# A mixture-of-experts kernel's first gather taken from fp32 rows, its router run stream by stream, and prefetch hints set ahead of its jumps

## The reference

```python
def hier_moe(h, w_coarse, w_fine, w1, w3, w2):
    x = h.reshape(b * l, d)
    p_coarse = softmax(x @ w_coarse)          # 4 groups
    p_g, g_sel = top_k(p_coarse, 1)           # one group for each token
    fine_g = (x @ w_fine).reshape(-1, 4, 8)[that group]   # 8 experts in it
    top_v, top_i = top_k(fine_g, 2)           # two experts for each token
    w_top = softmax(top_v) * p_g
    gates = ...                               # tokens x 32 experts, two entries a row
    hid = silu(x @ w1[e]) * (x @ w3[e])
    y = sum over e of (hid * gates[:, e]) @ w2[e]
```

## Time and profile before

| | us |
|---|---|
| median of 3 runs | 1395.68 (1394.09 to 1396.05) |
| the profiled execution, whole | 1395.73 |
| its span on the core | 1393.9 |
| MoE of layer 0, from the router's end to the last sum | about 369 to 705 |
| MoE of layer 1 | about 1043 to 1377 |
| PE busy | 1303.1 (93%) |
| DVE busy | 1001.1 (72%) |
| ACT busy | 737.4 (53%) |

### The profile page before, as it was taken

How to read it: one execution, slowest core, us unless ns; L and a number is a source line. 1 busy time by engine, 2 the same in 40 slices (tenths; PEclk the granted TensorE clock), 3 DMA queues, 4 the chain that set the end, 5 groups by cost and what they waited for, 6 DMA issues and landing times.

```text
span 1393.9 us, 17455 instructions
## 1 busy us (share of the span) xinstructions
PE 1303.1 (93%) x6480; PEld 1031.3 (74%) x6480; DVE 1001.1 (72%) x1130; ACT 737.4 (53%) x700; POOL 54.2 (4%) x89
## 2 busy tenths in 40 slices
PE   4999999999889999999979999999987999999994
PEld 1768777887677787887757777788776778788773
DVE  0646566677578888888877556666855888888887
ACT  1443453553456666667753444345434666676773
POOL 1300000001000000000020000000000000000000
PEclk8899999989879999999989999899986999999998
DMA  9977653326758999999966767343334899999991
GB/s 356 324 257 283 224 176 122 124 92 266 278 194 292 359 328 327 322 336 344 359 201 224 263 244 247 121 129 105 122 149 144 301 331 329 334 319 335 345 348 75
DMA packets 96563, 349.54 MB, mean 251 GB/s; under 512 B 8612, under 2 KB 12096, under 8 KB 80080
## 3 DMA queue, kind: packets, MB, share of 16 engines
q1 hardware_dynamic: 87504, 295.12, 59.7%
q0 software_dynamic: 8960, 53.16, 10.9%
HBM read 345.58 MB, written 3.70 MB: 251 GB/s over the span
## 4 chain that ended last, share of the span: by engine, by line
PE 71%; DVE 17%; DMA 4%; ACT 3%; issue 2%; DVEq 2%; SPq 1%; ACTq 0%
PE bank L863 67%; DVE wl L1687 9%; PE bank L866 4%; ACT wh L1597 2%; DMA raw<-in_moe_w 2%; DMA first<-in_w_ada 1%; DMA adaw<-in_w_ada 1%; DVE merged L1687 1%; DVE tmp L1687 1%; DVE x L1687 1%; DVE hid L2362 1%; SPq L708 0%; DVE gv L1687 0%; DVE xgl L2335 0%; DMA raw<-in_w_ada 0%
## 5 line engine op out<-in xcount | busy, mean ns | idle before, releaser
L1687 DVE TENSOR_TENSOR wl<-raw,wh 128x2048 fp32r<-128x2048 f32 (+1 forms) x268 | 610.4, 2278 | 148.5 <-ACT wh L1390 85.9
L1597 ACT ACTIVATE wh<-raw 128x2048 fp32r<-128x2048 f32 x192 | 367.4, 1916 | 62.7 <-PE bank L863 45.8
L863 PE MATMUL bank<-wh,xgh 128*128 128x512 f32 x512 | 213.7, 417 | 10.3 <-DVEq L2336 7.1
L863 PE MATMUL bank<-wh,xgl 128*128 128x512 f32 x512 | 206.1, 402 | 0.0
L863 PE MATMUL bank<-wl,xgh 128*128 128x512 f32 x512 | 205.7, 402 | 0.0
L863 PE MATMUL bank<-wh,hTh 128*128 128x512 f32 (+1 forms) x480 | 195.9, 408 | 9.5 <-ACT merged L1413 4.2
L1390 ACT ACTIVATE wh<-raw 128x2048 fp32r<-128x2048 f32 (+1 forms) x76 | 142.3, 1872 | 101.9 <-PE bank L863 62.1
L863 PE MATMUL bank<-wl,hTh 128*128 128x512 f32 (+1 forms) x480 | 191.2, 398 | 0.0
L863 PE MATMUL bank<-wh,hTl 128*128 128x512 f32 (+1 forms) x480 | 190.4, 397 | 0.0
L863 PEld LDWEIGHTS bank<-wh,xgh 128*128 128x128 f32 x512 | 99.2, 194 | 30.6 <-issue 11.0
L863 PEld LDWEIGHTS bank<-wh,hTh 128*128 128x128 f32 x480 | 94.8, 197 | 31.6 <-DVE wl L1687 5.9
(11 more groups left out here) (285 smaller groups left out, 1602.8 us busy)
## 6 DMA issues: line engine op xcount, KB each, us to landing
raw<-in_moe_w SPq DMA_DIRECT2D x256, 512.0 KB, 5.0
raw<-in_moe_w SPq DMA_DIRECT2D x64, 1024.0 KB, 6.1
raw<-in_w_in SPq DMA_DIRECT2D x52, 1024.0 KB, 6.5
adaw<-in_w_ada POOLq DMA_DIRECT2D x32, 1024.0 KB, 7.1
raw<-in_w_branch SPq DMA_DIRECT2D x12, 1024.0 KB, 5.2
raw<-in_w_ada SPq DMA_DIRECT2D x8, 1024.0 KB, 10.8
raw<-in_w_o SPq DMA_DIRECT2D x8, 1024.0 KB, 4.9
first<-in_w_ada SPq DMA_DIRECT2D x4, 1024.0 KB, 16.8
```

The source lines that it names most:

```text
L863: return behind(nc.tensor.matmul(*args, **kw))
L1597: tally(A_(wh[c][:, :], raw[:, r, :], ACT.Copy), part_high[c])
L1687: return V.tensor_tensor(o, a, b, op)
```

## The change

Three things. **The first gather**: ACT copies the turned-back rows as fp32 into a new tile `x2` (it overlaps `ygh`, `ygl`, not yet in use), PE gathers group 0 from `x2` with fp32 matmuls (16, in two steps, one for each half of the channels), ACT rounds the gathered bank into `xgh` and DVE subtracts it from the same bank into `xgl`. up(0) waits for each half apart. `x2h` is then copied from `x2` by ACT behind the gather, and `x2l` is written by DVE inside experts 1 and 2; the gathers of groups 1 to 3 use them as before. DVE's `lower` of piece 0 moves from ahead of the router to behind `selg`, ACT's `convert` of piece 1 moves ahead of the jump, and DVE lowers piece 2 ahead of expert 0's `hid`. **The router** multiplies half of stream 0 before stream 1 is turned, and both `turn_back`s come ahead of the rank matmuls. **The hints**: `rounds` is written with explicit jumps, each with a prefetch hint some instructions ahead of it (three experts ahead of the end on PE and ACT, ahead of the router's copy on DVE).

```diff
+FIRST_GATHER = {0: (UP_BANK, 0), 1: (TURN_BANK, 0), PREP - 1: (SUM_BANK, 0)}
+        LATE = 3
@@ rounds
             if straight:
-                with eng.If(more < 1):
-                    stream(single, 0, True)
-                with eng.Else():
-                    both()
+                eng.br_cond(more < 1, one, two)
+                one_round()        # ends: leave = eng.br(done); leave.branch_hint(single.late)
+                two_rounds()
             else:
...
+                eng.br_cond(more > 0, two, one).branch_hint(early)
+                two_rounds()
+                one_round()
@@ PE
                 next_ada(2, 6)
+                bank_free(pe, l, "rt")
+                pe.wait_ge(s0_act, 3 * l + 2)
+                route(0, 0, 4)
                 turn_x(l, "x2T", (1,))
                 next_ada(6, 8)
+                pe.wait_ge(s0_act, 3 * l + 3)
+                route(0, 4, 8)
+                pe.wait_ge(s1_dve, 2 * l + 2)
+                route(1, 0, 4)
+                pe.wait_ge(s1_act, 2 * l + 2)
+                fills(route(1, 4, 8), "rt")
                 turn_back(0)
+                turn_back(1)
                 pe.wait_ge(onehot_ready, l + 1)
...
                 fills(ins, "rank")
-                turn_back(1)
@@ PE, gather
+                    if g == 0 and j < 2 and rnd == 0:
+                        pe.wait_ge(x2_rows, 4 * l + 3 + j)
+                        for i in range(4):
+                            for s in range(2):
+                                a = x2[:, s, (4 * j + i) * P:(4 * j + i + 1) * P]
+                                ins = mm(bank[b][:, i * P:(i + 1) * P], a, selg[:, s, :].bitcast(F32), start=s == 0, stop=s == 1)
@@ PE, up
-                        if e == 0:
-                            pe.wait_ge(xg_act, N_G.moe(l, rnd, g) * 2 + 2)
-                            pe.wait_ge(xg_dve, N_G.moe(l, rnd, g) * 2 + 2)
                         for h in range(2):
+                            if e == 0:
+                                pe.wait_ge(xg_act, N_G.moe(l, rnd, g) * 2 + h + 1)
+                                pe.wait_ge(xg_dve, N_G.moe(l, rnd, g) * 2 + h + 1)
@@ ACT
-                        A_(x2h[:, s, h * 512:(h + 1) * 512], t[:, :], ACT.Copy).then_inc(x2_high, 1)
+                        frees(A_(x2[:, s, h * 512:(h + 1) * 512], t[:, :], ACT.Copy), f"x2{s}{h}")
+                        act.drain().then_inc(x2_rows, 1)
+                convert(Tally(act), 0, 1)
...
                     gathered(0, 0)
                     gathered(0, 1)
-                    piece(1)
+                    piece(2)
                     if rnd == 0:
+                        for s in range(2):
+                            A_(x2h[:, s, :], x2[:, s, :], ACT.Copy)
+                            act.drain().then_inc(x2_high, 1)
                         grown(1)
-                    piece(2)
@@ DVE
-                lower(Tally(dve), 0, 0)
+                early = dve.mark_branch_hint_location()
                 t = bank_full(dve, l, "rt")
...
                 choose(0, 0).then_inc(sel_ready, 1)
-                for s in range(2):
-                    for h in range(2):
...
-                        frees(tt(x2l[:, s, hs], t[:, :], x2h[:, s, hs].bitcast(F32), ALU.subtract), f"x2{s}{h}")
+                lower(Tally(dve), 0, 0)
...
+                        if g == 0 and j < 2:
+                            dve.wait_ge(xg_act, N_G.moe(l, rnd, 0) * 2 + j + 1)
+                            tally(tt(xgl[0][part], bank[b][:, :].rearrange("p (c t) -> p c t", c=4), xgh[0][part].bitcast(F32),
+                                     ALU.subtract), free[b])
+                            tally(drain(), xg_dve)
...
+                    gathered(0, 0)
                     piece(1)
-                    gathered(0, 2)
-                    gathered(0, 3)
+                    gathered(0, 1)
                     if rnd == 0:
                         finish_routing()
                         weigh(tally, 0)
+                        piece(2)
                     gathered(0, 4)
@@ DVE, expert i
+                        if rnd == 0 and i in (1, 2):
+                            s = i - 1
+                            dve.wait_ge(x2_high, 2 * l + s + 1)
+                            tt(x2l[:, s, :], x2[:, s, :], x2h[:, s, :].bitcast(F32), ALU.subtract)
+                            drain().then_inc(x2_ready, 1)
```

More of the change, by code:

```diff
@@ L273, in turn_order @@
 def turn_order():
-    order = [("gather", 0, 1), ("gather", 0, 3)]
+    order = [("gather", 0, 1)]
     for i in range(NE):
@@ L401, in hybrid_backbone @@
         (q, k, v, uTh, uTl, gate1, z, u, gv, gate, merged,
[L402 removed]
+         first0, first1, first2, first3, adaw0, adaw1, x2, x2h, x2l, xgh0, xgl0, ygh, ygl, selg, selT0, selT1, hTTh0, hTTl0, sil, hid) = region(
             "mixer_rows", 40,
@@ L639, in rounds, with one_round, two_rounds @@
             single, first, second = Tally(eng, counts), Tally(eng), Tally(eng)
-            def both():
-                stream(first, 0, False)
-                begin(second, 1)
-                stream(second, 1, True)
+            one, two, done = [f"{who}_{l}_{name}" for name in ("one", "two", "done")]
+            def one_round():
+                with nc.body(one, valid_engines=[eng.engine]):
+                    stream(single, 0, True)
+                    leave = eng.br(done)
+                    if straight:
+                        leave.branch_hint(single.late)
+            def two_rounds():
+                with nc.body(two, valid_engines=[eng.engine]):
+                    stream(first, 0, False)
+                    begin(second, 1)
+                    stream(second, 1, True)
+                    eng.br(done)
             if straight:
-                with eng.If(more < 1):
-                    stream(single, 0, True)
-                with eng.Else():
-                    both()
-            else:
-                with eng.If(more > 0):
-                    both()
-                with eng.Else():
-                    stream(single, 0, True)
+                eng.br_cond(more < 1, one, two)
+                one_round()
+                two_rounds()
+            else:
+                eng.br_cond(more > 0, two, one).branch_hint(early)
+                two_rounds()
+                one_round()
+            nc.switch_bb(done)
             for s, n, m in counts:
@@ L1209, in next_ada, with route, turn_back @@
                             accumulate(l, "ada_next", ("ada", l + 1, 0, c))
+                rt = bank[USE[l]["rt"][0]]
+                def route(s, first, end):
+                    for c in range(first, end):
+                        ins = mm(rt[:, s * 36:s * 36 + 36], merged[:, s, c * P:(c + 1) * P], rw[:, c, :], start=c == 0, stop=c == DC - 1)
+                    return ins
+                def turn_back(s):
+                    for h in range(2):
+                        turn4(l, f"x2{s}{h}", [merged[:, s, (4 * h + i) * P:(4 * h + i + 1) * P] for i in range(4)])
                 next_ada(0, 2)
```

82 lines of the change are left out of this document (42 added, 40 removed).

## The result

The changed kernel took 1383.66 us (median of 8, 1378.17 to 1389.70) against 1391.91 us (median of 8, 1386.27 to 1396.05) for the kernel before on the same chip: ratio 0.9946, 95% interval 0.9923 to 0.9970. Two later series on other chips gave 0.9903 (0.9883 to 0.9923) and 0.9930 (0.9904 to 0.9957). So it is faster, by 0.7% over the three, some 10 us. The executions of one series lie up to 13 us apart, and the medians of the changed kernel's three series 3.9 us. Of the 4.6 us between it and the forecast of 1388.3, 3.8 are that the kernel before measured 1391.91 and not the 1395.68 that the prediction was set against; the rest is the change, which won 8.3 us in this series, and 10 over the three, for 7.4 forecast.

A forecast was written before the change was run, and what follows sets the result against it. PE was taken as full in layer 0's later experts, so gains lay in the chain from gather to expert 1: (5.6 - 1.6) + (5.0 - 1.6) = 7.4 off 1395.73, 1388.3 us. Range 1386 to 1390.5; 8 in 10, 1384.5 to 1392.5.

The forecast's parts named there:

- T: Moment the selection is ready (selg's end): 373.75 us in layer 0, where selg had ended at 374.94; 1049.0 in layer 1.
- T to expert 1: From the selection through gather, expert 0 and routing to PE's start of expert 1: 19.3 us in both layers.
- expert 1 to the end: Rest of each layer's experts, where DVE now writes x2l: 1.6 us lost a layer, bounds 0 and 2.7.
- the hint is worth 0.1: DVE's jump ahead of the first xgl: unhinted xgl at T + 6.3 for T + 4.4, but a later wait hides it.
- the give-back: x2l on DVE in experts 1 and 2: of 2.7 us, 1.1 vanish in waits and 1.6 are lost a layer.
- The gather: First gather in fp32 on PE: 0.215 us a record at the low clock, halves done by T + 3.65 and T + 7.15.
- (a): Gather at the high clock, 0.112 us a record: steps 1.7 us earlier, 3.4 us more a layer, 1381.5 us; chance 0.12.
- The new wait: In the routing DVE stands 1.6 us for ACT's exponential, behind ACT's piece 2 and both x2h copies.
- Expert 1: PE's start of expert 1: 393.05 for 398.62 in layer 0, 1068.3 for 1073.32 in layer 1; late starts gone.
- (b): The shift is lost downstream because weights already flow near the DMA's limit; 1392 us if half is lost; chance 0.14.
- (c): The change does nothing: hid(0) held by something unmoved, or T later through ACT's drains of x2; 1395 us; chance 0.10.
- (d): Hints on PE and ACT disturb instruction fetch, 3.9 us a refetch: gain cancelled, or 1404 us with ACT; chance 0.07.

The follow-up runs named there:

- no_hints: The changed kernel without any prefetch hint, same jumps: 1385.49 us, ratio 0.9939.
- pad30: The changed kernel with 30 idle drains at the very start of DVE's program: 1381.88 us, ratio 0.9927.
- hint_at_rank: The changed kernel with DVE's hint 21 instructions later in both layers, ahead of the wait for the ranks: 1388.57 us, ratio 0.9970.
- hint_layer1: The changed kernel with DVE's hint in layer 1 alone, at its old place: 1387.29 us in one run.
- moved182_at_rank: The changed kernel with DVE's hint 21 instructions later and 182 never-run drains in layer 0's arm of two rounds: 1390.27 us, one run.
- place_a: The changed kernel with 20 idle drains at the start of DVE's program and 157 that never run: 1386.12 us, one run.
- place_c: The changed kernel with 18 idle drains at the start of DVE's program and 164 that never run: 1382.75 us, one run.
- after: The changed kernel as it is, in three series: 1383.66 us, ratio 0.9946; 1379.78 us, 0.9903; 1381.71 us, 0.9930.
- dve_hint_only: The changed kernel with the hints on DVE alone, none on PE and ACT: 1383.83 us, ratio 0.9937.
- moved150: The changed kernel with 12 idle drains at DVE's start and 138 never-run ones in layer 0's arm of two rounds: 1384.20 us, ratio 0.9956.
- moved203: The changed kernel with 203 never-run drains in DVE's layer 0 arm of two rounds: 1378.63 us, ratio 0.9904; again 1376.61 us, 0.9895.
- place_b: The changed kernel with 16 idle drains at DVE's start, 180 never-run ones, and layer 1's hint later, ahead of the ranks' wait: 1382.76 us, one run.
- before_hints: The kernel before with the explicit jumps and all six hints, nothing else of the change: 1392.37 us, ratio 0.9995.
- after_again: The changed kernel measured once more, on another chip: 1379.78 us, ratio 0.9903.

## Why the prediction was right and wrong

**The sum was near, its parts were not.** Forecast were 7.4 us, a ratio of 0.9947, and the first series has 0.9946; that this agrees is luck. By the marks of the profile before and the first one after (expert 1 is its start on PE):

```
us won                    layer 0              layer 1
                     forecast  measured   forecast  measured
T                       1.3      1.8         0.0      0.3
T to expert 1           4.3      6.2         5.0      3.0
expert 1 to the end    -1.6     -0.6        -1.6     -0.6
sum                     4.0      7.4         3.4      2.7
```

The seven profiles in which no hint of DVE helps (no_hints, pad30, hint_at_rank, hint_layer1, moved182_at_rank, place_a, place_c) have A to end at 679.4 to 684.5, mean 681.1: 5.5 us won. The five with layer 0's alone (after three times, dve_hint_only, moved150) have 676.6, 10.1 won; the three with both (moved203 twice, place_b) 672.8, 13.9. The mean ratios of the same groups (0.9945, 0.9934, 0.9900, of 3, 5 and 2 series) say 7.6, 9.1 and 14.0 us of 1392: between the first two groups they show 1.5 us where the profiles show 4.6, and they can't tell these apart.

**The step that failed: "the hint is worth 0.1".** It rests on the price of the jump, "up to 3.9 us", and on xgl at T + 6.3 unhinted. Unhinted it is at T + 8.3 to 8.6, 6.0 to 6.3 us behind the piece's end, and the hint moves it to T + 4.1: hid(0) comes at T + 16.4 for 20.3 to 20.9, and 3.8 us are left at the end of layer 0, by the means of the profiles with and without a working hint. For the old order both the price and the claim were right (before_hints: ratio 0.9995). I carried the old price into the new order, where piece 0 is lowered just ahead of the jump and a load of 1 MB stands in the way of the fetch: 2.2 us more. The sum had no such term, and layer 1, where the hint did not help, came 2.0 us short of it.

**Why the time lies below the range.** That error alone would have made the kernel slower than forecast. It was outweighed by three terms of the sum that were mis-sized the other way: T to expert 1 in layer 0 won 1.9 us more than the sum had, with the gather at the high clock and the wait for the exponential, put at 1.6, gone; the give-back, put at 1.6 a layer, was 0.6; and T came 0.8 better over both layers. To this come 3.8 us of the base, below.

**T.** Layer 0 was to come 1.3 us earlier and came 1.8 (14.30 to 12.53), and put back alone the lowering is worth 3.2; layer 1, 0.3 for 0.0. The step was right in kind, and 0.5 short in layer 0.

**The gather.** The price of an fp32 record was the row of gv, two for a matmul, and that held: 0.119 at the full clock. (The row's 1.95 us over 16 records are 0.122, and not the 0.112 of the prediction; only rival (a) and one bound use it.) The 14.6 us that the prediction gave beside it did not come: the 16 matmuls took 3.8 to 6.8. In layer 0 rival (a), the high clock, came true in 11 of the 18 profiles of the new order (first xgh 2.25 to 2.28 behind T); in layer 1 never (3.6 to 3.8). But 1.7 us a step did not go through, as (a) had it: in after_again layer 0 gathered at the low clock (xgh at 3.99 and 6.80), the first xgl came 0.6 later and hid(0) 0.95, 17.34 for 16.39, since DVE's own chain binds. Even hinted, the reading of need and the jump take 1.80 us behind the piece, for which the prediction had a handover of 0.1, so expert 1 comes at T + 17.4 and not at (a)'s T + 15.9.

**The new wait** for ACT's exponential was sized at 1.6 us. Where the gather is fast, the exponential waits for DVE, and DVE does not stand; in after_again it does. ACT in the first profile, then DVE in after_again:

```profile
379.37 0.21 ACT L1647 ACTIVATE rtr<-rtr 128x2 f32<-128x2 f32 x1 [1.01 <-DVEq L2331]
385.14 0.16 DVE L2335 TENSOR_REDUCE rtr<-rtr 128x2 f32<-128x8 f32 x1 [0.75 <-ACT rtr L1647]
```

0.75 us, half the forecast. Where the jump is unhinted it hides the wait altogether.

**Expert 1** was to start at T + 19.3. In the changed kernel T is 369.53 and 1042.24, so it starts at T + 17.4 and T + 21.3: 1.9 early where the hint works, 2.0 late where not. The waits for wl ahead of it (1.35 and 1.91) are gone, as forecast: hid(1) follows hid(0) by 10.96 and 10.12 for 13.26 and 12.20.

**Given back** were to be 1.6 us a layer. From hid(1) to the end the changed kernel takes 296.77 and 295.18, the old one 295.92 and 294.60: 0.85 and 0.58 (0.60 and 0.64 from expert 1's start on PE). The doubled subtraction shows that DVE passes such work on (2.2 and 4.1 for 2.6), so the work was not priced too high; that something else in this stretch won part of it back is likely and was not separated.

**Rivals.** (b) did not show: nothing more than that is lost. (c) did not happen in any series. (d) did not happen: with the hints at the ends of rounds the experts are not slower (after_again and dve_hint_only differ by 0.8 us in A to end); that mark ends ahead of those jumps in each layer, and the medians, 4.1 us apart the other way, don't settle what the hints win there. That a hint which fails costs nothing is shown by layer 1, 8.43 with it and 8.56 without.

**The base.** Of the distance from 1388.3 to 1383.66, 3.8 us are that the kernel before ran at 1391.91 in that series, with 1392 to 1394 in the longer ones. A range for a time, and not for a ratio, has to hold that scatter too; mine did not.

## What to carry to other kernels

Price a jump together with what the DMA does at that moment: on DVE it took 2.8 us behind the branch with the DMA idle and 5 with a load of 1 MB just issued, and an edit that moves work in front of a jump can move such a load there too. A prefetch hint is not a switch that is on when it is written: look behind the branch in the profile for each place, and if there are some 5 us of "issue", shift hint and jump along the stream until one of the marks, 128 instructions apart on DVE here, lies between them, the jump well behind it. Instructions in an arm that is not taken do this at no cost. Work that DVE does ahead of a short serial chain (the router) can be worth more than its own length when it moves into a wait behind it: 3.2 us for a piece of 2.3, by the one profile that put it back.

## What the hardware showed that I had not expected

DVE's unhinted jump over an arm stands 4.97 us behind its branch with weights in flight, 2.81 with the DMA idle, and 0.54 hinted; at the end of the round DVE is idle for 4.54 and 3.29 us for 0.2. Whether a hint of DVE helps depends on places in the stream to within two instructions (62 helps, 64 does not), so that 12 idle instructions left a hint whole, 18 undid it, and 203 that never ran switched another on.
